# Recurrence of a two-block layer: the spread of the keys' norms stands one turn further on in TensorE's program

## The reference

```python
def rwkv7_branch(feat, z, ...):
    f = token_shift(feat, mu_shift)
    r, k, v, wd, ad = split_cols(f, [512, 512, 512, 64, 64])
    w = exp(-DECAY_SCALE * sigmoid(w0 + tanh(wd) @ w_decay_up))
    a = sigmoid(a0 + ad @ w_iclr_up)
    kk = k * k_k
    kk = kk / maximum(norm(kk, axis=-1), 1e-12)        # one norm for each token and head
    k = k * (1.0 + (a - 1.0) * k_a)
    # S: a 64 x 64 state for each head, token by token
    S = S * w_t + (S @ -kk_t) (kk_t * a_t)^T + v_t k_t^T
    y_t = S @ r_t
    ...                                                # group norm, bonus, gate, w_out_a
```

## Time and profile before

| | us |
|---|---|
| median of 3 runs | 1895.66 (1895.03 to 1895.91) |
| the profiled execution, own time | 1894.98 |
| its span in the trace | 1893.2 |
| PE busy | 1828.9 (97%) |
| DVE busy | 953.0 (50%) |
| ACT busy | 793.1 (42%) |
| POOL busy | 410.1 (22%) |

### The profile page before, as it was taken

The page is one execution under the profiler, slowest core; times in us unless marked ns, Lnnn a source line. Parts: engine busy times, 40 slices in busy tenths (PEclk is TensorE's granted clock), DMA queues, the critical chain, the costliest instruction groups (busy, mean ns, idle before and its releaser), DMA issues.

```text
span 1893.2 us, 37184 instructions
## 1 busy us (share of the span) xinstructions
PE 1828.9 (97%) x15473; PEld 1478.4 (78%) x15473; DVE 953.0 (50%) x2056; ACT 793.1 (42%) x1725; POOL 410.1 (22%) x416
## 2 busy tenths in 40 slices
PE   6999999999999999999999999999999999999998
PEld 6997766888887789777777778777777786667887
DVE  5677766233344353135554465544653347774523
ACT  5346666343454343223343333333432346654421
POOL 4550000111213421312222222222221301001321
PEclk9999999999999999999999999999999999999999
DMA  5153310334323332330221222212113221005442
GB/s 189 38 170 95 86 40 1 103 99 129 103 87 106 112 134 89 108 106 27 85 60 50 68 67 62 75 50 81 61 42 99 76 64 46 1 1 175 148 156 89
DMA packets 145903, 159.81 MB, mean 84 GB/s; under 512 B 15076, under 2 KB 123944, under 8 KB 145736
## 3 DMA queue, kind: packets, MB, share of 16 engines
q1 hardware_dynamic: 145512, 156.44, 25.9%
q0 software_dynamic: 224, 0.99, 0.1%
HBM read 110.53 MB, written 52.62 MB: 86 GB/s over the span
## 4 chain that ended last, share of the span: by engine, by line
PE 89%; ACT 4%; DVE 3%; POOL 2%; DMA 2%; issue 1%; POOLq 0%; DVEq 0%; SPq 0%; ACTq 0%
PE ps L992 8%; PE ps L994 7%; PE ps L993 7%; PE ps L695 7%; PE ps L697 7%; PE ps L696 7%; PE ps L1103 4%; PE ps L805 3%; PE ps L784 3%; PE ps L884 3%; PE ps L886 3%; PE ps L885 3%; PE ps L792 3%; PE ps L1289 3%; PE ps L1140 3%; PE ps L1312 2%
## 5 line engine op out<-in xcount | busy, mean ns | idle before, releaser
L2809 POOL TENSOR_TENSOR t<-t,t 128x512 fp32r<-128x512 f32 x183 | 240.2, 1325 | 868.2 <-ACT t L1416 855.0
L992 PE MATMUL ps<-t,t 128*128 128x512 f32 (+2 forms) x720 | 293.0, 407 | 3.6 <-issue 2.3
L695 PE MATMUL ps<-t,t 128*128 128x256 f32 (+2 forms) x872 | 283.0, 325 | 3.1 <-issue 1.6
L696 PE MATMUL ps<-t,t 128*128 128x256 f32 (+2 forms) x872 | 277.1, 318 | 0.0
L697 PE MATMUL ps<-t,t 128*128 128x256 f32 (+2 forms) x872 | 277.1, 318 | 0.0
L994 PE MATMUL ps<-t,t 128*128 128x512 f32 (+2 forms) x720 | 269.6, 374 | 0.0
L993 PE MATMUL ps<-t,t 128*128 128x512 f32 (+2 forms) x720 | 269.4, 374 | 0.0
L695 PEld LDWEIGHTS ps<-t,t 128*128 128x128 f32 x872 | 166.5, 191 | 19.7 <-issue 8.4
L696 PEld LDWEIGHTS ps<-t,t 128*128 128x128 f32 x872 | 166.7, 191 | 10.3 <-issue 0.4
L697 PEld LDWEIGHTS ps<-t,t 128*128 128x128 f32 x872 | 166.4, 191 | 10.4
L992 PEld LDWEIGHTS ps<-t,t 128*128 128x128 f32 x720 | 137.0, 190 | 32.5 <-issue 9.9
(11 more groups left out here) (277 smaller groups left out, 3272.6 us busy)
## 6 DMA issues: line engine op xcount, KB each, us to landing
t<-in_w_in SPq DMA_DIRECT2D x53, 512.0 KB, 5.9
zgate_spill<-t SPq DMA_DIRECT2D x20, 512.0 KB, 3.1
tile_bias<-t SPq DMA_DIRECT2D x16, 576.0 KB
t<-tile_bias SPq DMA_DIRECT2D x8, 1152.0 KB, 6.3
t<-zgate_spill SPq DMA_DIRECT2D x16, 512.0 KB, 4.3
feat_spill<-t SPq DMA_DIRECT2D x13, 512.0 KB, 3.2
tile_bias<-band_bias SPq DMA_DIRECT2D x48, 128.0 KB
t<-values_and_gates SPq DMA_DIRECT2D x96, 64.0 KB
```

Source lines behind the costliest of these rows:

```text
L695: e.matmul(dst, lh, rh, start=k == 0, stop=False)
L696: e.matmul(dst, lh, rl, start=False, stop=False)
L992: e.matmul(dst, lh, rh, start=k == 0, stop=False)
L2809: e.tensor_tensor(WLO[wslot(b)][:, o], WST[:, o], WHI[wslot(b)][:, o].bitcast(F), ALU.subtract).then_inc(w_lo.sem, w_lo.up((b, p)))
```

## The change

One line of PE's `unit` moves: the `yield` that stood behind `head_spread("kk", ...)` now stands ahead of it. The spread of the keys' norms is thus in PE's turn 5 and no longer in turn 4. The number of turns, what is yielded in each, the waits of the spread itself, its bank in PSUM and the group norm's spread stay as they were.

```diff
@@ -1048,8 +1048,8 @@
                 yield STAGE_US
                 head_sums(E2, prep_a[u, "kk2"], "kk")
                 yield STAGE_US
+                yield STAGE_US
                 head_spread("kk", (prep_v, (u, "kn")))
-                yield STAGE_US
                 yield STAGE_US
                 yield STAGE_US
                 yield STAGE_US
```

## The result

| | before, us | after, us |
|---|---|---|
| median | 1895.68 (1895.03 to 1895.91, 4 runs) | 1883.69 (1882.40 to 1884.01, 4 runs) |
| the profiled execution, own time | 1894.98 | 1882.40 |
| its span | 1893.2 | 1880.5 |
| a second measurement, `after_again` | 1895.82 (15 runs) | 1883.29 (1882.47 to 1884.50) |

The changed kernel is faster. The ratio of the times is 0.9935 with an interval of 0.9923 to 0.9947, and 0.9938 (0.9925 to 0.9950) in the second measurement: 11.8 to 12.3 us less, where 9.4 us had been forecast. The range had ended at 1883.5 us, that is at a gain of 12.2; by the ratio the changed kernel takes 1883.3 us and lies just beyond it. The direction and most of the mechanism came out, the size was too small by a quarter.

A forecast was written before the change was run, and what follows sets the result against it. PE bounds the kernel, so its idle time counts, then its lower clock. 2.05 + 4.2 + 1.2 + 1.7 + 0.45 - 0.2 = 9.4 us off the median 1895.66 gives 1886.3 us; range 1883.5 to 1890.0.

The forecast's parts named there:

- unit 0: wait, clock and limit (2.05 + 1.7 - 0.2): Unit 0's spread: three trios cover 2.05 us of waiting, full clock returns 1.7, DVE's later work costs 0.2.
- unit 1, line 1190: PE's chain in unit 1 waits 1.4 us for POOL's memset; `gy` coming sooner gains 0.45 us.
- units 3, 5, 11, 12: The spread's waits for POOL's copy in these units, 4.2 us together, go entirely.
- unit 6: At unit 6's spread a wait of 0.25 us for DVE's line 2524 replaces 1.48; gain 1.2 us.
- The term of -0.2: Unit 0, line 1073: PE comes sooner but DVE's line 2465 does not; cost 0.2 us.
- In the other ten units PE finds the copy made, or nearly so.: Units outside 0, 3, 5, 6, 11 and 12 have no wait at the spread to remove.
- the collision of DVE and POOL: Rival: DVE's keys' product meets POOL's weights part in other units; two or more worse 0.11, better 0.06; 1.8 us each.
- nothing moves there: Units 7 and 13: their spread had no wait, so their meetings of DVE and POOL stay.
- The rival "better": Units 7 and 13 fall out of the pattern of DVE and POOL meeting: 1882.8 us; chance 0.06.
- a wait of 1.8 us in unit 7 that left the clock at 1.00: Evidence that unit 0's remaining 1.4 us keeps the clock up, giving back 1.7 us; rival of lost clock 0.12.
- the rival "slower": The spread's readers on DVE come late and delay line 1073 in all 16 units: 14.4 us, 1900.7 us; chance 0.03.

The follow-up runs named there:

- e3_waiting: Kernel before, with the spread moved one turn only in units 3, 5, 6, 11 and 12; 1891.92 us, ratio 0.9977.
- e4_others: Kernel before, with the spread moved only in units 1, 2, 4, 7, 8, 9, 10, 13, 14 and 15; 1895.89 us, ratio 0.9997.
- e1_unit0: Kernel before, with the spread moved one turn in unit 0 alone; 1893.05 us, ratio 0.9982.
- e7_two_trio: Kernel before, spread in its old turn, with two trios of the large product brought ahead of it in unit 0; 1895.14 us, ratio 0.9998.
- e6_one_trio: Kernel before, spread in its old turn, with one trio of the large product brought ahead of it in unit 0; 1893.73 us, ratio 0.9991.
- e5_two_more: Changed kernel, with two more trios of the large product ahead of the moved spread in every unit but unit 0; 1890.21 us, ratio 0.9969.

## Why the prediction was too small

| step | forecast, us | shown by the trace, us |
|---|---|---|
| unit 0: wait, clock and limit (2.05 + 1.7 - 0.2) | 3.55 | 3.62 |
| unit 1, line 1190 | 0.45 | 0.41 |
| units 3, 5, 11, 12 | 4.2 | 4.72 |
| unit 6 | 1.2 | 1.37 |
| units 8, 9, 13, 14, 15 | 0 | 1.21 |
| units 2, 4, 7, 10 | 0 | -0.03 |
| sum | 9.4 | 11.30 |

The forecast is 1.9 us short: 1.2 us in units that it had put at nothing, 0.5 in units 3, 5, 11 and 12, 0.2 in unit 6. Unit 0 and unit 1 came out.

**Unit 0: the wait and the clock right.** The wait left is 1.41 us for a forecast of 1.4; the clock came back and gave 3.62 - 2.05 = 1.57 us for a forecast of 1.7. The term of -0.2 was too large: line 1073 starts 838.26 - 824.07 = 14.19 us behind the sums before and 833.30 - 822.77 = 10.53 after, 3.66 sooner, so that only 0.04 us were passed on.

**Unit 1, the wait for the memset: right.** The memset releases line 1190 at 871.17 - 861.56 = 9.61 us behind the sums before and at 865.83 - 856.64 = 9.19 after, 0.42 sooner. The wait shrinks by less, 1.43 to 1.13 us, because PE comes there 0.12 sooner too.

**Units 3, 5, 6, 11 and 12: the right waits, each counted too small.** The prediction took the numbers in brackets for the price: 0.79, 1.46, 1.46 and 0.52 us in units 3, 5, 11 and 12. The steps are 0.85, 1.54, 1.56 and 0.77, so 0.06 to 0.25 more; unit 6 gave 1.37 for 1.2. The brackets are counted from the modelled end of the matmul before, and matmuls overlap: front to front, the spread behind a wait lay further behind its predecessor than bracket and normal distance say. `e3_waiting` shows the five alone: 6.1 us against 4.2 + 1.48 = 5.7 of idle time in the earlier trace rows.

**The step that failed: "In the other ten units PE finds the copy made, or nearly so."** The argument put them at zero. They gave 1.2 us beside unit 1's 0.41, and `e4_others`, where they stand alone, gave the same 1.6. Half of the 1.2 us was waiting at the spread after all: 0.18 us in unit 9, 0.17 in unit 15 and 0.26 of unit 14's 0.43 (there it is 0.38 us from line 994 to the spread where 0.23 is usual, and 0.55 on to line 1140 where 0.44 is). For unit 9 the rows show how. The plan's first part and the spread behind it, kernel before, first in unit 7, then in unit 9:

```profile
1102.45 0.69 PE L1172 MATMUL ps<-t,t 64*64 64x64 f32 x32
...
1103.07 0.71 PE L1032 MATMUL ps<-t,t 128*128 128x128 f32 x4
```

```profile
1180.90 0.69 PE L1172 MATMUL ps<-t,t 64*64 64x64 f32 x32
...
1181.70 0.71 PE L1032 MATMUL ps<-t,t 128*128 128x128 f32 x4
```

and the kernel after in unit 9, where a trio follows:

```profile
1171.70 0.69 PE L1172 MATMUL ps<-t,t 64*64 64x64 f32 x32
...
1172.32 0.50 PE L992 MATMUL ps<-t,t 128*128 128x512 f32 x1
```

From one start to the next it is 0.62 us in unit 7, 0.80 in unit 9, and 0.62 after. The row of unit 9 has no bracket and PE counts as busy throughout; yet 0.18 us of waiting lie in it, just the unit's step. Waits of 0.15 to 0.18 us don't show in the rows of the matmuls. They do show, in the trace of the kernel before too, in those of the weight load (PEld), which goes ahead of the matmul. Its waits at the spread, and at line 1172, from 815 to 1484 us before:

```profile
PEld ps L1032 <- POOL t L2961: 12.7, 11, 3.8
...
PEld ps L1172 <- DVE t L2524: 1.4, 3, 0.5
```

The list has eleven places at the spread where that of the matmuls has seven: units 1, 9, 14 and 15 are the four more. After the change it has two (2.6 us).

**Units 8 and 14: another wait, which the prediction didn't have.** The rest of unit 14's gain (0.16 us) and all of unit 8's (0.15) were not lost at the spread. They stood at the plan's first part, whose weight load waited for DVE's last step on line 2524, kernel before, unit 8:

```profile
1143.76 0.56 PEld L1172 LDWEIGHTS ps<-t,t 64*64 64x64 f32 x32 [0.52 <-DVE t L2524]
```

From line 994 to line 1172 it is 0.48 us from start to start in these two units, and 0.32 in the other even ones. Now the spread stands between the two, PE does it while DVE finishes, and the bracket is gone.

**Unit 13** (0.28 us) has a third cause, and here the collision of DVE and POOL comes in. The wait at line 1073 and what stands ahead of it, kernel before:

```profile
1346.02 1.30 POOL L2809 TENSOR_TENSOR t<-t,t 128x512 fp32r<-128x512 f32 x1 [4.21 <-ACT t L1416]
...
1346.21 1.39 DVE L2456 TENSOR_TENSOR t<-t,t 128x256 f32<-128x256 f32 x1
...
1350.43 0.67 PE L1073 MATMUL ps<-t,t 128*128 128x256 f32 x2 [1.74 <-DVE t L2463]
```

and after:

```profile
1334.01 1.29 POOL L2809 TENSOR_TENSOR t<-t,t 128x512 fp32r<-128x512 f32 x1 [3.92 <-ACT t L1416]
...
1334.47 1.11 DVE L2456 TENSOR_TENSOR t<-t,t 128x256 f32<-128x256 f32 x1
...
1338.42 0.67 PE L1073 MATMUL ps<-t,t 128*128 128x256 f32 x2 [1.47 <-DVE t L2463]
```

POOL's part starts 0.46 us ahead of DVE's product instead of 0.19, so DVE stands for 0.28 us less, and PE's wait is 1.47 us and not 1.74. It starts sooner by the same path that shortened unit 1's wait: `gy` comes sooner by the spread's length, so ACT's line 1726, behind its copy of `gy`, starts 6.78 us behind the unit's sums and not 7.08, and the rounding and POOL's part follow. The prediction had this path for unit 1 alone. Of unit 13 it said that "nothing moves there", because its spread had no wait; that was wrong. The wait is 1.46 or 1.47 us in all kernels that move this unit's spread by the one turn alone and leave line 1073 as it is, and 1.74 in all that don't. The rival "better" had a unit drop out of the meeting; what happened is a part of that in one of the two units. DVE's product ends 0.28 us behind POOL's part in both kernels (1346.21 + 1.39 = 1347.60 and 1346.02 + 1.30 = 1347.32; 1334.47 + 1.11 = 1335.58 and 1334.01 + 1.29 = 1335.30), which is the shape that the Trainium skill, SBUF — State Buffer, section "Who interferes with whom", gives: whoever comes second stands until the first is done.

**The clock: right in unit 0, wrong in its argument.** The prediction leaned on a wait of 1.8 us in unit 7 that left the clock at 1.00. The same wait was followed by a half clock in unit 7 in `e1_unit0`, `e4_others` and `e7_two_trio`, and the like wait of unit 13 in `e3_waiting`; in the other traces it was not. One trace of one wait had shown one of two outcomes. The Trainium skill, TensorE: Matmul & The Clock Gate, table "Why this matters for your kernels", allows gaps up to some 3 us; `e6_one_trio` with 2.75 us and these waits of 1.8 us lie beneath that, and lost the clock. The 1.4 us of the change was far enough down in every trace.

**Readers of the spread, and the rival "slower".** No cost in the change itself, as forecast: lines 2531 and 2545 of DVE still wait for PE after the change:

```profile
1098.44 0.22 DVE L2545 TENSOR_TENSOR t<-ps,t 128x64 f32<-128x64 f32 x1 [0.55 <-PE ps L1191]
...
1135.32 0.76 DVE L2531 TENSOR_TENSOR t<-ps,t 128x256 f32<-128x256 f32 x2 [0.23 <-PE ps L1172]
```

They had 0.59 and 0.15 us of idle time before. `e5_two_more` shows how near the edge is in the even units.

**The transfer from trace to time.** The traces give 11.3 us for the recurrence, the runs 11.8 to 12.3. The difference lies within the intervals of the ratios. Clock is a likely part of it: the mean granted clock is 0.9949 in the 15 runs of the kernel before that stand beside `after_again` and 0.9968 in its five, 0.0019 apart, where the 3.4 us of unit 0 make 0.0009. So the runs of the kernel before have more half clock in the mean than its trace. The longer one of unit 0 (6.8 us) stands in one of the five traces with the old form, and so explains little of it; where the rest falls stays open.

## What to carry to other kernels

Price a wait from start to start, against a place where the same pair of instructions runs undisturbed, and in every unit: here the forecast missed 1.9 of 11.3 us, a sixth of the gain, and most of that lay in waits that the matmuls' rows don't show or show too short. The rows of the weight load show them, so that their list of waits belongs beside that of the matmuls. Independent work ahead of a waiting instruction is worth its own length, and where a half clock stands behind the wait, its 1.6 us come on top at once when the wait becomes short enough. Then the same means belongs on the next waits (lines 1073 and 1218 gave another 8.4 to 8.8 us; line 1190 gave next to nothing, for the wait came back at the unit's line 1073), not further on at the same place, where the next reader becomes late (`e5_two_more`, 6.5 to 7 us worse).

## What the hardware showed that had not been expected

- The half clocks behind waits of 1.74 to 3.4 us in the recurrence lasted 3.4 us each, and once 6.8 us (`e4_others`, unit 0). One of 3.4 us cost 1.55 to 1.65 us; that of 6.8 us cost 1.23 more and not 1.6, since it began while PE was idle.
- Whether it comes behind a wait of TensorE of 1.5 to 2.3 us differs between executions: four times in the 20 waits of 1.46 to 1.80 us that ten traces have at line 1073 in units 7 and 13, ten times in 13 behind the 2.30 us near 764 us, twice in 13 behind waits of 1.50 to 2.19 us at line 695. Behind the 1.41 us of unit 0 it never came (six traces), behind 2.52 us (one trace), 2.75 us (one trace) and 3.43 us (five traces) it came each time. One trace therefore doesn't tell what a wait of 1.5 to 2.5 us costs. The mean granted clock of many runs tells more.
- DVE's product beside POOL's part of the weights takes 1.39 or 1.11 us, by 0.27 us in how far ahead of it POOL starts, and 0.42 in unit 7 of `e5_two_more`, where DVE starts first.
